# Where four operand tiles of the matmuls begin in SBUF, modulo 256 bytes

## The reference

```python
def swiglu_ffn(x, norm, w_gate, w_up, w_down):
    h = rms_norm(x, norm)
    return (jax.nn.silu(h @ w_gate) * (h @ w_up)) @ w_down

for l in range(DEPTH):                                  # 2 layers
    x = x + 0.5 * swiglu_ffn(x, ...)
    h = rms_norm(x, mix_norm[l])
    aq, ak, av, bq, bk, bv, cq, ck, cv, cg, gates = jnp.split(h @ w_in[l], split_points, axis=-1)
    ...                                                 # three attentions, gates, projections
    x = x + merged @ w_out[l]
    x = x + 0.5 * swiglu_ffn(x, ...)
...                                                     # second block: h @ w_in, scan, @ w_out
    x = x + gf_x * rms_norm_2(swiglu(hx2, w_gate[l], w_up[l], w_down[l]), g_post_ffn[l])
```

## Time and profile before

| | |
|---|---|
| runs of the kernel | 1677.86, 1679.23, 1679.37 us, median 1679.23 |
| span of the profiled execution | 1675.5 us |
| median less that span | 3.7 us |
| PE busy | 1639.3 us, 98% |
| PEld busy | 1566.5 us, 93% |
| DVE, ACT, POOL busy | 73%, 55%, 12% |

### The profile page before, as it was taken

The page is one execution under the profiler, slowest core; times in us unless marked ns, Lnnn a source line. Parts: engine busy times, 40 slices in busy tenths (PEclk is TensorE's granted clock), DMA queues, the critical chain, the costliest instruction groups (busy, mean ns, idle before and its releaser), DMA issues.

```text
span 1675.5 us, 30692 instructions
## 1 busy us (share of the span) xinstructions
PE 1639.3 (98%) x13558; PEld 1566.5 (93%) x13558; DVE 1221.6 (73%) x1369; ACT 914.6 (55%) x1096; POOL 208.0 (12%) x127
## 2 busy tenths in 40 slices
PE   7999999999999999999999999999999999989997
PEld 7999988999999999999987899999999988879997
DVE  7656678678876667766678678785899598685654
ACT  6444556675554454544465685464555557454543
POOL 1000100000130001200010000042323358300000
PEclk9999999999999999999999999999999999999999
DMA  7666654444566665667654434555554433235551
GB/s 274 231 251 254 233 185 167 151 152 151 196 235 227 251 229 198 230 227 263 234 197 167 160 137 153 189 207 193 182 199 177 150 112 139 76 114 190 200 195 57
DMA packets 45779, 315.53 MB, mean 188 GB/s; under 512 B 5328, under 2 KB 6096, under 8 KB 8272
## 3 DMA queue, kind: packets, MB, share of 16 engines
q1 hardware_dynamic: 45648, 313.58, 51.6%
HBM read 312.51 MB, written 1.05 MB: 187 GB/s over the span
## 4 chain that ended last, share of the span: by engine, by line
PE 89%; DVE 7%; ACT 2%; DMA 1%; issue 1%; SPq 0%; POOL 0%; POOLq 0%; DVEq 0%
PE ps L1165 24%; PE ps L1167 24%; PE ps L1166 24%; PE ps L1354 3%; PE ps L1356 3%; PE ps L1355 3%; DVE wlo L1788 2%; PE ps L1136 1%; PE ps L1368 1%; DVE pre L2369 1%; DMA raw<-in_w_dram 1%; PE ps L1379 1%; DVE dA_rows L1788 1%; DVE tmp L1788 1%; DVE qkA L1788 1%
## 5 line engine op out<-in xcount | busy, mean ns | idle before, releaser
L640 ACT ACTIVATE whi<-raw 128x2048 fp32r<-128x2048 f32 x265 | 503.7, 1911 | 302.2 <-DMA raw<-in_w_dram 302.0
L1788 DVE TENSOR_TENSOR wlo<-raw,whi 128x2048 fp32r<-128x2048 f32 (+1 forms) x251 | 581.3, 2324 | 112.6 <-ACT whi L640 108.3
L1165 PE MATMUL ps<-h1hi,whi 128*128 128x256 f32 x1792 | 504.3, 281 | 9.0 <-DVE wlo L1788 9.0
L1166 PE MATMUL ps<-h1hi,wlo 128*128 128x256 f32 x1792 | 498.3, 278 | 0.0
L1167 PE MATMUL ps<-h1lo,whi 128*128 128x256 f32 x1792 | 498.2, 278 | 0.0
L1165 PEld LDWEIGHTS ps<-h1hi,whi 128*128 128x128 f32 x1792 | 338.3, 189 | 14.0 <-DVE wlo L1788 9.0
L1166 PEld LDWEIGHTS ps<-h1hi,wlo 128*128 128x128 f32 x1792 | 338.3, 189 | 0.1
L1167 PEld LDWEIGHTS ps<-h1lo,whi 128*128 128x128 f32 x1792 | 338.0, 189 | 0.0
L1165 PE MATMUL ps<-hid_hi,whi 128*128 128x256 f32 x880 | 244.1, 277 | 0.3 <-DVE hid_lo L1788 0.3
L1166 PE MATMUL ps<-hid_hi,wlo 128*128 128x256 f32 x880 | 243.4, 277 | 0.0
L1167 PE MATMUL ps<-hid_lo,whi 128*128 128x256 f32 x880 | 243.4, 277 | 0.0
(11 more groups left out here) (351 smaller groups left out, 2551.5 us busy)
## 6 DMA issues: line engine op xcount, KB each, us to landing
raw<-in_w_dram SPq DMA_DIRECT2D x289, 1024.0 KB, 4.8
raw<-in_w_dram SPq DMA_DIRECT2D x4, 512.0 KB, 7.0
relbias<-in_relbias_dram SPq DMA_DIRECT2D x2, 1024.0 KB, 7.0
pv<-in_pv_dram SPq DMA_DIRECT2D x2, 641.0 KB, 5.9
xT<-in_x_dram SPq DMA_DIRECT2D x4, 256.0 KB, 5.5
ctxT<-in_ctx_dram SPq DMA_DIRECT2D x1, 1024.0 KB, 6.9
out_dram<-xT SPq DMA_DIRECT2D x4, 256.0 KB, 2.5
decay<-in_decay_dram SPq DMA_DIRECT2D x1, 512.0 KB, 10.7
```

The costliest lines, as they stand in the source:

```text
L640: act.activation(whi[:, slot, :], raw[:, slot, :], ACT.Copy).then_inc(hi_done[slot], 1)
L1165: pe.matmul(out, w_hi, hi, start=start, stop=False, skip_group_check=skip)
L1166: pe.matmul(out, w_lo, hi, start=False, stop=False, skip_group_check=skip)
L1788: return dve.tensor_tensor(out, a, b, op)
```

## The change

Only addresses change. `hhi`, and with it `hlo`, begins 96 bytes later, at 32 modulo 256. What follows up to `rscale` moves along by 96 bytes. The next call of `operand_base` had 96 bytes to fill before and has none now, so that all from `gate_sig` to `pT` stays where it was, `hid_hi`, `hid_lo` and `yT_hi`, `yT_lo` among them. Then 32 bytes are put in ahead of `h1hi`: `h1hi`, `h1lo` and all behind them move by 32 bytes.

| tiles | begin modulo 256, before | now |
|---|---|---|
| `raw`, `wlo`, `whi` (weight rings), `xT` | 0 | 0 |
| `hhi`, `hlo`; over them `m_hi`, `m_lo`, `vA`, `vB`, `vC`, `gC` | 192 | 32 |
| `ident`, `ones` | 192 | 32 |
| `t_gate`, `t_up`, `t_exp`, `t_hid`, `merged`, `score1`, `rscale` | 64 | 160 |
| `gate_sig`, `qkA`, `qkB`, `hid_hi`, `hid_lo`, `sq`, `yT_hi`, `yT_lo`, `qkT`, `pT` | 192 | 192 |
| `h1hi`, `h1lo`; over them `xdt`, `mix_g`, `gated`; `pv` | 192 | 224 |
| `cosg`, `sing`, `decay`, `small`, `ctxT` | 224 | 0 |

The instructions of every engine, their order and their waits are the same as before.

```diff
-    hhi0 = operand_base()
+    operand_base()
+    base[0] += 96
+    hhi0 = base[0]
     hhi = sb("hhi", [P, KT, S], F32R)
     hlo = sb("hlo", [P, KT, S], F32R)
...
-    for first in (hhi0, g0, a0, c0, t0, base[0]):
+    assert hhi0 % 256 == 32
+    for first in (g0, a0, c0, t0, base[0]):
         assert first % 256 == 192, first
...
+    base[0] += 32
     v0 = base[0]
-    assert v0 % 256 == 192
+    assert v0 % 256 == 224
     h1hi = sb("h1hi", [P, KT, S], F32R)
     h1lo = sb("h1lo", [P, KT, S], F32R)
...
-    assert d0 + 12288 == v0
+    assert d0 + 12288 <= v0
```

## The result

The changed kernel takes 1710.82 us (median of 4 runs, 1710.16 to 1711.58), against 1679.03 us before. The ratio on record is 1.0181, with a 95% interval of 1.0162 to 1.0200; the two medians by themselves give 31.8 us more, 1.0189, inside the interval. It is clearly slower. I had forecast 1670 us and a range up to 1705 us.

What follows compares the result with a forecast made beforehand. PE's pace was taken as the bound: span 1675.5 - 9.4 (slow stretches) + 0 (other engines) + 0 (fast pace) = 1666.1 us, plus 3.7 us from span to median, 1669.8, said as 1670 us; range 1662 to 1705 us.

Steps and rivals of the forecast that it cites:

- The bound: Whole kernel: PE is busy for 98% of the span, so nothing counts but the pace of PE.
- ACT, DVE and POOL don't mind 32 bytes: Reads and writes of moved tiles by these engines: 32 bytes off a multiple of 64 costs nothing seen, entered at 0.
- The fast pace itself: PE's 113.35 ns a matmul, on moved tiles: no change, entered at 0; bounds 39 us less and 52 us more.
- My own sign of being wrong: PE on moved tiles: forecast wrong if the pace is a third value, neither 113.3 nor 117.7 ns.
- The slow pace: PE stretches at about 117.7 ns a matmul, 2129 matmuls: changing address relations would end them, -9.4 us.
- The slower side: Whole kernel: slower by over 0.2%, summed over several rivals; chance 0.31.
- The slow pace takes over: Rival: all 7824 matmuls on moved tiles run at 117.7 ns, 25 us more, 1704 us; chance 0.12.
- the loss per block changes: Rival: PE's loss per 64 bytes of moving row changes on moved tiles, 1640 or 1731 us; chance 0.05 each way.
- The rule of the Trainium skill: SBUF reads: lines of 16 bytes, each row covering as many as before, so the sum would be 0, not -9.4 us.

Runs made afterwards that it cites:

- e6_weights_192: Kernel before with only the weight rings (and `xT`, `gains_all`) moved 64 bytes down, to 192 modulo 256; 1734.17 us, ratio 1.0328.
- e10_wlo_192: Kernel before with only the ring of the low weights (`wlo`, and `raw` on it) moved, to 192 modulo 256; 1726.63 against 1679.58 us, ratio 1.0272.

## Why the prediction was wrong

**The bound.** Right: PE's pace alone sets the end, and the time moved with it. Also right was that ACT, DVE and POOL don't mind 32 bytes (entered at 0, measured within 1.2 us).

**The fast pace itself, entered at 0.** This step failed. It measured +4.9 ns on `h1hi` (118.2 less 113.35) and +3.3 ns on `hhi` (116.6 less 113.35), inside the bounds of -5 and +6.7 ns, which I gave and then set aside. The reason for 0 was that moving rows at 0 and at 192 had about the same pace. That comparison looked at one start at a time. In the turned products the slab at 0 moves past a stationary block at 192, a difference of 64; in the others it is 192 less 0. The rows thus compared two differences, in two kinds of product whose tables differ, and said nothing of 224 or 32 in either. My own sign of being wrong came true: the pace on moved tiles is a third value (and a fourth).

**The slow pace, entered at -9.4 us.** This failed too, and with the wrong sign for `hid_hi`; my bounds of 0 and -9.4 us left no room for a loss. The pace does hang on the relation between the two starts, as I wrote, but a change of relation between tiles doesn't break the slow one. PE comes from `h1hi` at 224 to `hid_hi` at 192 and is in the slow pace there (72 to 76 us). By the means of the groups, 277 and now (280 + 279 + 278)/3 = 279 ns, between 276 for fast and 281 for slow, the slow share on `hid_hi` went from about 0.2 to 0.6. That is 0.4 x 2640 x 4.4 ns = 4.6 us of the loss, an estimate from rounded means. (For the second and third of these three means, see the groups of lines 1170 and 1171:)

```profile
L1170 PE MATMUL ps<-hid_hi,wlo 128*128 128x256 f32 x880 | 245.3, 279 | 0.0
L1171 PE MATMUL ps<-hid_lo,whi 128*128 128x256 f32 x880 | 245.1, 278 | 0.0
```

**The size.** Over the pace of before, which is 113.35 ns and 4.39 ns more for 2129 of 11040 matmuls (the 10464 and 576 on `yT_hi` and `yT_lo`), 114.2 ns on average, `h1hi` at 118.2 ns loses 5376 x 4.0 = 21.5 us, and `hhi` and `m_hi` at 116.6 ns lose 2448 x 2.4 = 5.9 us. To this come 4.6 us on `hid_hi`. On `yT_hi` and `yT_lo`, whose means rose from 276 to 279 ns, it is by the same estimate 0.6 x 576 x 4.4 = 1.5 us. On the turned products, whose durations rose by 3 ns (396 to 399 on line 1354), it is 864 x 3 = 2.6 us (by their windows above, which are coarse, up to 864 x 5.3 = 4.6 us). The sum is 36.1 us, an estimate from rounded means, against 35.7 us more of busy PE and 34.2 us between the two profiled spans.

**The rivals.** The slower side had 0.31. "The slow pace takes over", at 1704 us, was the nearest in size and wrong in kind, since the paces are new ones. The right kind was "the loss per block changes", upwards, which had 0.05 and 1731 us; its doubled loss of 6.7 ns more on every moved tile was too much. The rule of the Trainium skill (Advanced Engine Details and Errata, SBUF Cachelines), read as no effect because all starts are multiples of 16, doesn't tell these cases apart: the measurements go from 1679 to 1740 us with starts that are all multiples of 32. The Trainium skill, SBUF — State Buffer, Who interferes with whom, gives PE two read ports, one for the moving operand and one for the weight load, and calls them independent. In this case's runs the pace does depend on both addresses: moving the weight rings (with `xT` and `gains_all`), with every moving tile in its place, costs up to 55 us (`e6_weights_192`).

What is shown is that in `block3` the difference between the two starts sets the pace: shifting both together changes nothing, shifting either alone does. That the two reads get in each other's way inside SBUF is a reading; no run measured it, and `e10_wlo_192` doesn't decide it. Open are also the period of the pattern (256 bytes or more), why 192 is the best and 64 mostly slow, why the turned products have another order, and what picks between two paces at a restart.

## What to carry to other kernels

In a kernel that PE bounds with `fp32r` matmuls of 256 columns and a weight load each, choose the start of the moving tiles in relation to that of the weight tiles, and keep it the same for all of them: between the best and the worst of eight differences lie 61 us of 1679 here. Measure the differences for each kind of matmul in the kernel, as the turned products here rank them in another way. Divide the length of a dense window by its count of matmuls to see it, as no wait or idle time shows. When two rows of a trace seem to say that an address doesn't matter, write down both operands' addresses before believing it.

## What the hardware showed that I had not expected

- Shifting all of SBUF's contents by 32 bytes changes nothing (1.0007), shifting operands without weights by the same 32 bytes costs 2.5% (1.0255).
- For `block3` the differences of 96 and 0 bytes are the worst (120.0 ns a matmul) and 192 is the best (113.4 ns). For the turned products 0 is the best of the four looked at (226.8 ns) and 192 is slow (232.0 ns).
- At a difference of 192 in `block3` PE has two paces, 113.35 and 117.7 ns, and keeps one through hundreds of matmuls. With four small matmuls put in ahead of it, a stretch of 56 us went from the slow to the fast, and another, of 15 us and more, from the fast to the slow.
